# Spreading the scan's decay sums by transfer, and its modulation rows over four TensorE column groups

## The reference

```
a_cs = jnp.cumsum(a, axis=2)
seg = a_cs[:, :, :, None] - a_cs[:, :, None, :]
decay = jnp.exp(jnp.where(lower, seg, -jnp.inf))
cb = jnp.einsum('bctgn,bcsgn->bctsg', cc, bc)
y_diag = jnp.einsum('bctsgh,bcsghp->bctghp', cb[..., None] * decay, xdt)
...
y_off = jnp.einsum('bctgn,bcghpn->bctghp', cc, h_in) * jnp.exp(a_cs)[..., None]
```

## Time and profile before

| | us |
|---|---|
| median of 3 runs | 1659.67 (1658.86 to 1660.76) |
| the profiled execution, its time | 1660.72 |
| its span, first to last instruction | 1659.0 |
| the loop's first and last DVE step in it | 731.3 and 975.7 |

### The profile page before, as it was taken

How to read it: one execution, slowest core, us unless ns; L and a number is a source line. 1 busy time by engine, 2 the same in 40 slices (tenths; PEclk the granted TensorE clock), 3 DMA queues, 4 the chain that set the end, 5 groups by cost and what they waited for, 6 DMA issues and landing times. The chain is left out here.

```text
span 1659.0 us, 21834 instructions
## 1 busy us (share of the span) xinstructions
PE 1436.3 (87%) x8577; PEld 1273.0 (77%) x8577; DVE 815.5 (49%) x897; ACT 621.9 (37%) x1007; POOL 276.0 (17%) x278
## 2 busy tenths in 40 slices
PE   3999989799999999699999954999984489999980
PEld 1789989799997889568888843998873378888860
DVE  2411532476672111264443349233346089999966
ACT  3423311244432221223333437111031177777753
POOL 0600000000000010247766632000004100000002
PEclk9899999899999999799999976999966699999985
DMA  9972211121213331521111121322434589999945
GB/s 388 403 297 77 77 51 51 60 77 53 75 52 131 120 139 42 167 65 39 40 38 40 39 104 75 133 93 76 183 152 179 205 317 404 407 412 413 406 182 202
DMA packets 55500, 268.04 MB, mean 162 GB/s; under 512 B 7467, under 2 KB 11763, under 8 KB 35062
## 3 DMA queue, kind: packets, MB, share of 16 engines
q1 hardware_dynamic: 42806, 221.21, 35.2%
q0 software_dynamic: 12608, 45.62, 7.1%
HBM read 218.54 MB, written 48.27 MB: 161 GB/s over the span
## 5 line engine op out<-in xcount | busy, mean ns | idle before, releaser
L212 PE MATMUL banks<-rounded,rounded 128*128 128x320 f32 (+1 forms) x1168 | 366.5, 314 | 20.1 <-DVE rounded L735 6.7
L213 PE MATMUL banks<-rounded,rounded 128*128 128x320 f32 (+1 forms) x1168 | 364.5, 312 | 0.0
L214 PE MATMUL banks<-rounded,rounded 128*128 128x320 f32 (+1 forms) x1168 | 364.3, 312 | 0.0
L212 PEld LDWEIGHTS banks<-rounded,rounded 128*128 128x128 f32 (+1 forms) x1168 | 221.4, 190 | 21.6 <-issue 14.1
L191 DVE TENSOR_TENSOR rounded<-words,rounded 128x2048 fp32r<-128x2048 f32 x52 | 119.2, 2292 | 226.4 <-ACT rounded L183 224.2
L1827 DVE TENSOR_TENSOR rounded<-words,rounded 128x2048 fp32r<-128x2048 f32 x93 | 212.9, 2290 | 34.4 <-ACT rounded L1818 33.8
L213 PEld LDWEIGHTS banks<-rounded,rounded 128*128 128x128 f32 (+1 forms) x1168 | 221.5, 190 | 0.5
L214 PEld LDWEIGHTS banks<-rounded,rounded 128*128 128x128 f32 (+1 forms) x1168 | 221.4, 190 | 0.4
L1818 ACT ACTIVATE rounded<-words 128x2048 fp32r<-128x2048 f32 x96 | 183.7, 1917 | 48.3 <-PE banks L1945 40.8
L1136 ACT ACTIVATE words<-banks,words 128x128 f32<-128x128 f32 x320 | 89.4, 370 | 178.5 <-PE banks L1042 178.5
L183 ACT ACTIVATE rounded<-words 128x2048 fp32r<-128x2048 f32 x52 | 99.2, 1908 | 140.1 <-PE banks L233 62.1
(11 more groups left out here) (267 smaller groups left out, 2229.4 us busy)
## 6 DMA issues: line engine op xcount, KB each, us to landing
words<-in_units SPq DMA_DIRECT2D x52, 1024.0 KB, 4.9
words<-in_wg SPq DMA_DIRECT2D x32, 1024.0 KB, 7.8
words<-in_wu SPq DMA_DIRECT2D x32, 1024.0 KB, 7.9
words<-in_wd SPq DMA_DIRECT2D x32, 1024.0 KB, 8.7
words<-in_w_mod_rest SPq DMA_DIRECT2D x32, 512.0 KB, 5.1
slot_rows<-words POOLq DMA_DIRECT2D x27, 512.0 KB, 22.2
expert_rows<-words POOLq DMA_DIRECT2D x25, 512.0 KB, 9.7
words<-in_w_mod SPq DMA_DIRECT2D x4, 2048.0 KB, 22.6
```

The costliest lines, as they stand in the source:

```text
L212: nc.tensor.matmul(out, lhs[0](k), rhs[0](k), start=(k == 0), stop=False)
L213: nc.tensor.matmul(out, lhs[0](k), rhs[1](k), start=False, stop=False)
L214: last = nc.tensor.matmul(out, lhs[1](k), rhs[0](k), start=False, stop=(k == nk - 1))
```

## The change

**Decays by transfer.** `prepare` keeps only C·B. Once, at the stage's start, ten matmuls turn the running sums (heads on partitions), ACT copies them and issues sixteen transfers to a scratch in memory (`sums`). For each sub-tile SP loads 1024 sums broadcast to all 128 partitions (`spread`, 512 KB) straight into a slot of `E`, now four slots. ACT turns them into decays in two steps, eight `Relu` with bias and one `Exp` over 1024 columns. The masks, which came in through PE, are now on C·B: DVE makes two masked copies per group (`masks`). The timed rows `XT` have two slots instead of three, so POOL times the rows of j + 1, and does it after `finish_y(j - 1)`.

**Modulation over column groups.** The matmul k of a piece writes partitions 32·(k mod 4) onward of bank 0, with 32 columns of weights (2 and zeros). DVE copies the four partial rows to `MP` (`take_part`). A matmul with a selection matrix adds them, with the bias, in bank 1 (`add_parts`), and this is done when the next piece comes, just before its `modulate`; the row leaves by `take_modulation` at that same place. SP's load of piece i + 2 waits for the sum of piece i, and stands behind `spread`.

```diff
-    E = kit.at(O_HL + 2048, 6, 512)
-    XT = kit.at(O_HL + 5120, 6, 256)
+    E = kit.at(O_HL + 2048, SLOTS, 1024)
+    XT = kit.at(O_HL + 6144, 4, 256)
...
+            def spread(j):
+                c, g, q = subs[j]
+                n = (c * 2 * G + 2 * g + q) * 1024
+                if j >= SLOTS:
+                    sp.wait_ge(y_done, j - SLOTS + 1)
+                sp.dma_start(E[:, j % SLOTS, :], scr["sums"][:, n:n + 1024].partition_broadcast(P)).then_inc(sums_spread[j % SLOTS], 16)
...
+            for j in range(NS):
+                if j + SLOTS < NS:
+                    spread(j + SLOTS)
+                if j in at_sub:
+                    store_piece(at_sub[j] - 1)
+            store_piece(NP - 1)
...
-                if j + 2 < NS:
-                    time_rows(j + 2)
                 if 1 <= j < NL + 1:
                     finish_y(j - 1)
+                if 1 <= j < NS - 1:
+                    time_rows(j + 1)
...
-                for d, mask in ((0, le), (1, ge)):
-                    if j:
-                        pe.wait_ge(decays_done, 8 * j - 4 + 4 * d)
-                    nc.tensor.matmul(ps[:, d, :].rearrange("p (h n) -> p h n", h=4), identb,
-                                     shut[:, d, :].unsqueeze(1).broadcast_to([P, 4, P]), start=True, stop=False)
-                    for h in range(4):
-                        n = 32 * d + heads4(g, q).start + h
-                        last = nc.tensor.matmul(ps[:, d, h * P:(h + 1) * P], A[:, c, n:n + 1].broadcast_to([P, P]), mask,
-                                                start=False, stop=(h == 3))
-                    last.then_inc(sums_spread, 1)
...
+                for k in range(KD):
+                    part = 32 * (k % 4)
+                    last = nc.tensor.matmul(ps[part:part + 32, 0, 0:P], sc[:, k, :], WM[:, i % 2, k * P:(k + 1) * P],
+                                            start=(k < 4), stop=(k >= 4))
+                last.then_inc(mod_part, 1)
+
+            def add_parts(i):
+                pe.wait_ge(mod_copied, i + 1)
+                if i:
                     pe.wait_ge(mod_taken, i)
...
+            for d, mask in ((0, le), (1, ge)):
+                for c in range(NC):
+                    o = ps[32 * d:32 * d + 32, 2 + c // 4, (c % 4) * P:(c % 4 + 1) * P]
+                    last = nc.tensor.matmul(o, A[:, c, 32 * d:32 * d + 32], mask, start=True, stop=True)
+            last.then_inc(sums_turned, 1)
...
                 if j in at_sub:
-                    modulate(at_sub[j], min((j + 1) // 2, NS // 2 - 1) + 1)
+                    add_parts(at_sub[j] - 1)
+                    modulate(at_sub[j])
...
+            act.wait_ge(sums_turned, 1)
+            nc.scalar.activation(CS, ps[0:64, 2:4, :].rearrange("p a b -> p (a b)")[:, 0:T], ACT.Copy).then_inc(sums_taken, 1)
+            act.wait_ge(sums_taken, 1)
+            stored = scr["sums"][0].rearrange("(c s d h t) -> s d h c t", c=NC, s=2 * G, d=2, h=4)
+            for d in range(2):
+                for k in range(2 * G):
+                    act.dma_start(stored[k, d], CS[32 * d + 4 * k:32 * d + 4 * k + 4, :].rearrange("h (c t) -> h c t", c=NC)).then_inc(sums_stored, 16)
...
+                act.wait_ge(gaps_done, 8 * j + 8)
+                nc.scalar.activation(e, e, ACT.Exp, scale=-1.0).then_inc(decays_done, 1)
...
+            def masks(gi):
+                dve.wait_ge(cb_done, gi + 1)
+                src = ps[:, 4, (gi % 2) * P:(gi % 2 + 1) * P]
+                nc.vector.tensor_tensor(CB[:, gi % 2, 0, :], src, le, ALU.mult).then_inc(cb_masked, 1)
+                nc.vector.tensor_tensor(CB[:, gi % 2, 1, :], src, ge, ALU.mult).then_inc(cb_masked, 1)
+
+            masks(0)
             for j, (c, g, q) in enumerate(subs):
-                dve.wait_ge(cb_taken, j // 2 + 1)
-                dve.wait_ge(decays_done, 8 * j + 8)
-                e = E[:, 2 * (j % 3):2 * (j % 3) + 2, :].rearrange("p d (h t) -> p (d h) t", h=4)
-                nc.vector.tensor_tensor(e, e, CB[:, (j // 2) % 2, :].unsqueeze(1).broadcast_to([P, 8, P]),
+                if j % 2 and j + 1 < NS:
+                    masks((j + 1) // 2)
```

More of the change, by code:

```diff
@@ L908, in stage_ssd @@
     cond_loaded, cond_silu, mod_done, mod_taken = (kit.sem("s_" + x) for x in ("cond", "cond_silu", "mod", "mod_row"))
+    mod_part, mod_copied, sc_clear = (kit.sem("s_" + x) for x in ("mod_part", "mod_copied", "sc_clear"))
     mod_weights, mod_stored = ([kit.sem(f"s_{x}{j}") for j in range(2)] for x in ("mod_weights", "mod_stored"))
@@ L957, in _ @@
             sp.dma_start(DSK, io["d_skip"].partition_broadcast(P)).then_inc(states_loaded, 16)
+            sp.wait_ge(sums_stored, 16 * 16)
+            for j in range(SLOTS):
+                spread(j)
             for x, (d, c, g) in enumerate(ctx_states):
@@ L961, in _, with store_piece @@
                              SO[:, x % 2, :].rearrange("p (q n) -> p q n", q=4)).then_inc(state_stored[x % 2], 16)
-            for i in range(NP):
+            def store_piece(i):
+                if i < 0:
+                    return
                 if i + 2 < NP:
@@ L966, in _ @@
                 sp.dma_start(scr["mod"][:, P * i:P * (i + 1)], MR[0:2, i % 2, :]).then_inc(mod_stored[i % 2], 16)
+            for i in range(EARLY):
+                store_piece(i - 1)
+            for j in range(NS):
[4 more added lines that the diff above has]
+            store_piece(NP - 1)
             for j in range(2):
@@ L1047, in prepare, with modulate @@
                     if gi >= 2:
-                        pe.wait_ge(cb_taken, gi - 1)
-                    pe.wait_ge(mod_taken, EARLY + sum(i < j - 1 for i in at_sub))
+                        pe.wait_ge(cb_masked, 2 * (gi - 1))
                     nc.tensor.matmul(ps[:, 4, (gi % 2) * P:(gi % 2 + 1) * P], BT[:, g, c * P:(c + 1) * P],
                                      CT[:, g, c * P:(c + 1) * P], start=True, stop=True).then_inc(cb_done, 1)
-            def modulate(i, masked=0):
+            def modulate(i):
                 pe.wait_ge(mod_weights[i % 2], 32 * (i // 2 + 1))
                 if i:
-                    pe.wait_ge(mod_taken, i)
-                if masked:
-                    pe.wait_ge(cb_taken, masked)
-                o = ps[0:2, 4, 256 + (i % 2) * P:256 + (i % 2 + 1) * P]
-                for k in range(KD):
-                    nc.tensor.matmul(o, sc.rearrange("p (k s) -> p k s", s=2)[:, k, :], WM[:, i % 2, k * P:(k + 1) * P],
-                                     start=(k == 0), stop=False)
-                nc.tensor.matmul(o, kit.const("one")[0:1, 0:2], BM[0:1, i % 2, :], start=False, stop=True).then_inc(mod_done, 1)
+                    pe.wait_ge(mod_copied, i)
+                else:
+                    pe.wait_ge(exps_done, 4)
+                for k in range(KD):
[6 more added lines that the diff above has]
+                if i:
+                    pe.wait_ge(mod_taken, i)
+                nc.tensor.matmul(ps[0:2, 1, 0:P], sel, MP[:, i % 2, :], start=True, stop=False)
+                nc.tensor.matmul(ps[0:2, 1, 0:P], kit.const("one")[0:1, 0:2], BM[0:1, i % 2, :],
+                                 start=False, stop=True).then_inc(mod_done, 1)
             for n, (mask, d) in enumerate(sums):
@@ L1073, in _ @@
                 if x in early:
+                    if early[x]:
+                        add_parts(early[x] - 1)
                     modulate(early[x])
             pe.wait_ge(exps_done, 4)
-            pe.wait_ge(shut_ready, 3)
+            pe.wait_ge(sums_taken, 1)
             prepare(0)
@@ L1100, in _ @@
                     for d in range(2):
-                        b = 2 * (j % 3) + d
-                        last = nc.tensor.matmul(o, E[:, b, h * P:(h + 1) * P], XT[:, b, h * HD:(h + 1) * HD],
+                        at = d * 512 + h * P
+                        last = nc.tensor.matmul(o, E[:, j % SLOTS, at:at + P], XT[:, 2 * (j % 2) + d, h * HD:(h + 1) * HD],
                                                 start=(d == 0), stop=(d == 1))
                 last.then_inc(y_done, 1)
+            add_parts(NP - 1)
         @block.scalar
@@ L1142, in _ @@
         def _(dve):
-            for d, mask in ((0, le), (1, ge)):
-                nc.vector.tensor_scalar(shut[:, d, :], mask, BIG, -BIG, ALU.mult, ALU.add).then_inc(shut_ready, 1)
-            nc.vector.tensor_copy(identb, kit.const("ident")).then_inc(shut_ready, 1)
+            nc.vector.memset(sc, 0.0).then_inc(sc_clear, 1)
             dve.wait_ge(exps_done, 4)
@@ L1175, in _ @@
                 if x in early:
-                    take_modulation(early[x])
+                    take_part(early[x])
             weigh(dve, nc.vector, NX + 1)
```

66 lines of the change are left out of this document (37 added, 29 removed).

## The result

The changed kernel takes 1670.0 us (median of 5 runs, 1665.7 to 1675.4) where the kernel before takes 1659.7: a ratio of 1.0058, with a 95% interval of 1.0032 to 1.0084. It is slower, as forecast, but by 10 us and not by 34. The profiled execution took 1665.7.

A forecast was written before the change was run, and what follows sets the result against it. TensorE alone bound the loop before; after, its waits for GpSimd and DVE and a falling clock. Pairs +21.4 and +1.4, chunk 0 -1, start +10.5, states +2, first tile -3.5, joint +1, end +2.4: +34.2, so 1694 us, range 1640 to 1722.

The forecast's parts named there:

- The chain in a pair: Early pairs, from the start of y(j): DVE's product, then GpSimd's timing and weighting hold TensorE; next Z at 12.7 us.
- The ten pairs: Sub-tiles 0 to 19, early modulation: 15.4 us a pair with a falling clock in place of 13.26, +21.4 us together.
- the second hole: TensorE's wait for GpSimd's weighting before each state product, 2.85 us; work behind it expected at 1.2 GHz.
- The rest of the loop: The 5.5 pairs after the ten: 71.8 us against 70.4 before, +1.4 us.
- 14.0 taken: The two later pairs that still have states: 11.0 us at full clock, 16.9 low, 14.0 each assumed.
- 12.5 taken: Chunk 1 pairs, no state: 9.2 us, 13.4 with all TensorE work at 1.2 GHz, 12.5 each assumed.
- The 9.2: Chunk 1 pair from y(j), the piece's load landing 5.5 us later, modulation, cross-chunk products and a wake-up: 9.2 us.
- The start: Stage start to first y: +10.5 us before the exponentials, +2 in the state phase, -3.5 for the first tile.
- Chunk 0 and the end: Chunk 0 34 us, was 35.1 (-1); joint between chunks 1 and 0 +1; last piece's sum to landing +2.4.
- (b): Rival, whole loop: the clock holds, early pairs 12.7 us, kernel 1640 us; chance 0.17.
- (c): Rival, whole loop: short clock dips, early pairs 14.3 us, then 12.6 and 10.6, kernel 1668 us; chance 0.18.
- (e): Rival, loop: transfers late, 10 us to landing, all pairs 13.5 us, kernel 1685 us; chance 0.05.

The follow-up runs named there:

- e1: The changed kernel with GpSimd's weighting for the state product moved before the last addition of y(j-2): 1637.1 us, 0.9902 of before.
- e4: The changed kernel with three idle matmuls in each of the two holes of the twelve pairs with a state product: 1650.6 us.
- e5: The changed kernel with DVE's two carry instructions moved behind y(j)'s addition in the next turn: 1684.5 us.
- e10: The changed kernel with three idle matmuls only in the first hole of a pair, before y(j+1): 1666.0 us.
- e11: The changed kernel with three idle matmuls only in the second hole of a pair, before the state product: 1661.1 us.
- e2: The changed kernel with the 16 stores of the turned sums issued by SP in place of ScalarE: 1671.5 us.
- e12: e6 with the sums' stores on SP and the first four spreads issued behind the loads of modulation pieces 2, 3 and 4: 1615.8 us.
- e9: e6 with two idle matmuls ahead of each y of chunks 1 and 0: 1619.1 us.
- e3: The changed kernel with modulation rows made as before (16 matmuls and a bias in one accumulation, no column groups, no sum of parts): 1688.2 us.
- e6: The changed kernel with GpSimd's weighting early, DVE's carry behind y(j)'s addition and the masks behind the product: 1614.7 us, 0.9753 of before.
- e13: The changed kernel with one more GpSimd instruction ahead of the timed rows in each pair of chunk 1: 1678.0 us.
- e15: e9 with modulation weights of pieces 7 to 23 loaded only by half: chunk 0 30.3 us in place of 37.7 (whole 1648.3 us, other values).

## Why the prediction was right in sign and wrong in size

**The chain in a pair: right.** Forecast from Z: y(j+1) at 5.0, GpSimd's addition 5.9, timing 7.5, weighting 8.5, state product 9.6. Measured: 5.34, 6.2, 7.8, 8.8, 9.9. The holes are 2.31 us (2.1 forecast) and 1.3 to 2.4 (2.85, less where y(j+1) runs slower). A piece has a pitch of 0.57 us at full clock (804.18 to 804.75 in e1; 0.55 forecast), a sum of parts 0.6 (0.53).

**The ten pairs: right.** 15.05 us each (14.9 and 15.8 in turn), 15.4 forecast: 150.5 us and not 154. e4 shows 13.1 with the clock held, where 12.7 was worked out, and e5 17.0 with it low. What was not foreseen is where the clock falls. It was to fall behind the second hole; in the trace it falls in all ten pairs while y(j+1) runs, so behind the first one and before the second begins: 0.4 us after the start of 779.26, and at 766.0, 1.6 us after the start of 764.41. What is slow behind the second hole was slow before it. e10 and e11 show that either hole alone can bring a fall.

**The rest of the loop is the step that failed.** "14.0 taken" and "12.5 taken" for the pairs with a state and those of chunk 1, in sum +1.4 us against before. From y(20) to y(32) before took 76.7 us and the changed kernel 61.9: -14.8. That is 16 of the 24 us. The term that was mis-sized is the 12.5: the one pair here with a state, y(20) to y(22), took 16.4 us, near the prediction's low-clock end of 16.9, but the four behind it took 8.7 to 9.0 and the last 10.3. I carried the low clock of the ten pairs into pairs where there is no state product, hence no second hole, and the one hole is 1.1 to 1.3 us (rows of 913.42, 922.08 and 931.10). The clock stood at 1.00 from 900 to 930 us.

The 9.2 that the prediction had as its lower bound is near by luck: it was made of a wait for a piece's load, and that wait was at most 0.45 us there (row of 925.42), where GpSimd's timed rows, which it did not count, held y up by 1.32. The profile of before pointed to the low end, since no hole there is as long as the pause of 1.85 us that did no harm. But it did not prove it: the holes at 913.42 and 922.08 left the clock up, and behind the one at 931.10, just as long, it fell and stayed down to the end of the stage. So it is shown that the clock stayed up in chunk 1 and what that was worth; which pause brings it down stays open.

**The start was mis-sized, for a cause of its own.** Forecast for y(0) were +10.5, +2 and -3.5, together +9; measured +3.1. The first scale, and with it the exponentials, did come 9.0 us later (15.4 us after the stage's start against 6.5). But the next 44 us took 50 before. If decays not made before the first y are the -3.5, as I worked them out but did not measure, the other 2.4, with the +2 that didn't come, lie in the state phase, which I had put down to DVE's copies. e2 shows what bounds it: with the exponentials 5.9 us sooner y(0) stays, and e12 shows that the order of transfers on SP takes it 5.6 us down. That is 6 of the 24 us. How much of before's 50 us was slack I did not measure.

**Chunk 0 and the end**: 36.8 and the last piece's sum, 1.4 us more than before in all, where -1, +1 and +2.4 were forecast. Right, by compensation in part: at the low level TensorE is the bound, at the full one the loads.

**The rivals.** (b) would have needed the second hole gone; e1 takes it away and gives 1637, against its 1640, but the nearness is luck, since the clock still fell in e1 and its pairs differ. e4 is the better test of its price: where the clock did hold, a pair was 12.9 on average, against its 12.7. (c), at 1668, had the total but not its parts: the pairs were not 14.3, and chunk 1 was better than its 10.6. (e), late transfers, cost the loop of this kernel waits of under 0.7 us and play a part in that of e9. The Trainium skill (TensorEngine Tiling (Array Packing), Key Properties) says that changing the tiling mode drains the engine, and I had made 8 us of that as an estimate. The estimate is not borne out: 16 records four at a time are 0.46 us at least, a quarter of 1.84, and a piece's pitch is 0.57, so its two changes cost at most 0.11 together and not 0.34, under 3 us for all 24 pieces. e3, without column groups in its pieces, is 18 us slower.

## What to carry to other kernels

When an edit takes work from the busiest engine, look at what it moves on the engines that had slack: here the loss came from two instructions in another order on GpSimd. Moving the weighting turned +0.6% into -1.0%, and DVE's carry and masks after it into -2.5%. Price the clock stage by stage from the holes that remain in each, not from the worst stage, take the price as a range, and test it by filling a hole with idle matmuls: what gets faster with more work was paying for the clock. Two holes in one loop belong together; closing one may only widen the other.

## What was not expected of the hardware

- The pauses before a fall were not of one length: a hole of 2.31 us left the clock up once in e1 (800.75) and was followed by a fall four times; in the changed kernel two holes of 1.32 us left it up and a third was followed by a fall; in e6 and e13 it fell once among pauses of no more than 1.2 us.
- In chunk 0 the clock stayed at 0.50 with TensorE busy for 9.3 of 10 us and more, for 40 us, until the stage ended. With fillers in chunks 1 and 0 it was up for most of chunk 0 (e9, e15).
- The same GpSimd instruction of 256 columns took 0.72 us or 1.63 to 1.79, and the weighting 1.04 or 2.02 (e5), the longest ones where DVE's product ran beside it.
